# Where the exponentials of two softmax pairs stand on ScalarE, in the prompt tiles of a hybrid decoder layer

## The reference

```python
h = _rms_norm(x, p['ln_mix_pre'])
qa, ka, va, qkvb, bb, ab, zb, qc, gates = jnp.split(h @ p['w_in'], _split_points(), axis=-1)
oa, new_wk, new_wv = swa_fn(qa, ka, va)                       # window attention with sinks, 8 heads of 64
ob, new_conv, new_rec = _gdn_branch(qkvb, bb, ab, zb, ...)    # gated DeltaNet, 4 heads of 128
oc = _mem_attend(qc, mem_k, mem_v)                            # attention to 256 memory rows, 4 heads of 128
gate = jax.nn.sigmoid(gates.reshape(Bsz, L, N_BRANCH, D_MODEL))
mix = jnp.sum(gate * up, axis=2) @ p['w_out']
x = x + _rms_norm(mix, p['ln_mix_post'])
...                                                           # then a SwiGLU feed-forward part
```

## Time and profile before

| | |
|---|---|
| median of 3 runs | 2065.21 us |
| the runs | 2065.07, 2065.21, 2067.7 us |
| the profiled execution | 2062.75 us |
| its span, first to last instruction | 2060.9 us |
| mean granted TensorE clock, as a share of full speed | 0.997 |
| TensorE busy | 2002.7 us (97% of the span) |
| VectorE busy | 987.8 us (48%) |
| ScalarE busy | 517.7 us (25%) |
| GpSimd busy | 742.3 us (36%) |

### The profile page before, as it was taken

One profiled execution on the slowest core, in us unless ns is written; L12 is line 12 of the kernel. 1 busy time (PEld: TensorE's weight loads), 2 busy tenths in 40 slices (PEclk: granted clock), 3 DMA queues, 4 the chain that ended last, 5 costly groups with the idle time before them and its releaser, 6 DMA issues.

```text
span 2060.9 us, 36132 instructions
## 1 busy us (share of the span) xinstructions
PE 2002.7 (97%) x14350; PEld 1903.8 (92%) x14350; DVE 987.8 (48%) x1761; ACT 517.7 (25%) x1151; POOL 742.3 (36%) x318
## 2 busy tenths in 40 slices
PE   6999999999999999999999999999999999999998
PEld 6999999888888889989799888999999999999997
DVE  6755630356565555322459745434353525253535
ACT  5333621243343444321232333100000000000002
POOL 3434774222111122123145322443434343434344
PEclk9999999999999999999999999999999999999999
DMA  5223333433233332263674421111111111111114
GB/s 189 92 83 100 109 114 99 146 105 88 61 99 88 100 91 68 78 190 120 204 247 159 150 104 67 42 51 41 51 41 51 41 51 41 51 41 51 41 41 179
DMA packets 221294, 193.91 MB, mean 94 GB/s; under 512 B 24731, under 2 KB 192283, under 8 KB 221170
## 3 DMA queue, kind: packets, MB, share of 16 engines
q1 hardware_dynamic: 207058, 182.72, 28.7%
q10 hardware_dynamic: 14128, 9.65, 1.6%
HBM read 146.26 MB, written 47.09 MB: 94 GB/s over the span
## 4 chain that ended last, share of the span: by engine, by line
PE 91%; DVE 3%; DMA 2%; ACT 1%; issue 1%; SPq 1%; POOL 0%; ACTq 0%; DVEq 0%; POOLq 0%
PE psum L1508 24%; PE psum L995 13%; PE psum L1569 11%; PE psum L1200 9%; PE psum L1523 5%; PE psum L1500 4%; PE psum L1278 4%; PE psum L1112 3%; PE psum L1247 2%; PE psum L1183 1%; PE psum L1236 1%; PE psum L1019 1%; PE psum L1060 1%; PE psum L1186 1%; ACT pr L1846 1%
## 5 line engine op out<-in xcount | busy, mean ns | idle before, releaser
L853 POOL TENSOR_TENSOR wsp<-raw,kc 128x1024 fp32r<-128x1024 f32 x115 | 279.5, 2430 | 1101.6 <-PE psum L1200 391.6
L1508 PE MATMUL psum<-actD,wsp 128*128 128x352 f32 x3168 | 515.8, 323 | 1.0 <-ACT sg L2052 0.6
L1508 PEld LDWEIGHTS psum<-actD,wsp 128*128 128x128 f32 x3168 | 509.0, 188 | 1.6 <-issue 0.9
L856 POOL TENSOR_TENSOR wsp<-raw,wsp 128x1024 fp32r<-128x1024 f32 x115 | 283.7, 2467 | 9.0
L995 PE MATMUL psum<-actT,wsp 128*128 128x352 f32 x1656 | 269.6, 323 | 0.0
L2640 DVE TENSOR_TENSOR accT<-accT,psum 128x352 f32<-128x352 f32 x504 | 241.7, 520 | 50.1 <-PE psum L1569 50.1
L995 PEld LDWEIGHTS psum<-actT,wsp 128*128 128x128 f32 x1656 | 264.8, 188 | 0.3
L1569 PE MATMUL psum<-fT,wsp 128*128 128x352 f32 x1512 | 249.8, 323 | 0.4 <-DVE accT L2640 0.4
L1569 PEld LDWEIGHTS psum<-fT,wsp 128*128 128x128 f32 x1512 | 244.0, 188 | 0.7 <-DVE accT L2640 0.7
L1200 PE MATMUL psum<-actT,wsp 128*128 128x352 f32 x1152 | 229.6, 338 | 0.0
L2623 DVE TENSOR_TENSOR fr<-psum,sg 128x352 f32<-128x352 f32 x66 | 34.5, 524 | 375.3 <-PE psum L1508 373.1
(11 more groups left out here) (452 smaller groups left out, 2484.8 us busy)
## 6 DMA issues: line engine op xcount, KB each, us to landing
raw<-in_w_in SPq DMA_DIRECT2D x100, 256.0 KB, 4.0
raw<-in_w_ffn_in SPq DMA_DIRECT2D x88, 256.0 KB, 3.1
gat<-s_gate SPq DMA_DIRECT2D x12, 1056.0 KB, 5.0
raw<-in_w_ffn_out SPq DMA_DIRECT2D x44, 256.0 KB, 2.7
s_gate<-gst SPq DMA_DIRECT2D x48, 176.0 KB, 1.9
s_qkv<-y SPq DMA_DIRECT2D x12, 528.0 KB, 3.0
brw<-s_br SPq DMA_DIRECT2D x3, 2112.0 KB, 9.5
raw<-in_w_branch SPq DMA_DIRECT2D x24, 256.0 KB, 5.6
```

Of the source, the lines that this page charges most:

```text
L853: pool.tensor_tensor(wsp[:, slot, 0], raw[:, slot], ones.unsqueeze(1).to_broadcast([P, KT, P]), ALU.mult).then_inc(w_hi, 1)
L856: pool.tensor_tensor(wsp[:, slot, 1], raw[:, slot], wsp[:, slot, 0].bitcast(F32), ALU.subtract).then_inc(w_lo, 1)
L1508: mm = pe.matmul(psum[:, bank, 0:CH], wsp[:, slot, a, k, :], actD[:, h, k, CH * c:CH * c + CH], start=(k == 0 and q == 0), stop=(k == KT - ...
```

## The change

The exponentials of an S step get a step of their own, `("Z", j)`, and `act_tile` issues them there. `TILE` gets six Z steps. Z0, Z3, Z4 and Z5 stand directly behind S0, S3, S4 and S5. Z1 stands behind Y1, Z2 behind Y4. No other engine has a branch for Z. Of the tuple, the part with Z1 and Z2 (before with -, after with +):

```diff
-            ... "INV", ("G", 8), ("E", 0), ("S", 1), ("Y", 1), ("G", 4),
-            ("X", 1), ("G", 3), ("Y", 2), ("T", 1), ("X", 2), ("G", 3), ("Y", 3), ("V", 1), ("X", 3), ("S", 2), ("Y", 4), ("G", 4),
-            ("X", 4), ("G", 3), ("Y", 5), ("T", 2), ("X", 5), ...
+            ... "INV", ("G", 8), ("E", 0), ("S", 1), ("Y", 1),
+            ("Z", 1), ("G", 4), ("X", 1), ("G", 3), ("Y", 2), ("T", 1), ("X", 2), ("G", 3), ("Y", 3), ("V", 1), ("X", 3), ("S", 2),
+            ("Y", 4), ("Z", 2), ("G", 4), ("X", 4), ("G", 3), ("Y", 5), ("T", 2), ("X", 5), ...
@@ act_tile
                     if j == 0:
                         copy((a_vt, t + 1), vtok[:].rearrange("p a d -> p (a d)"), psum[:, 4, 0:2 * P], a_vc)
+                elif step[0] == "Z":
+                    j = step[1]
                     act.wait_ge(a_nm, 6 * t + j + 1)
                     for a in range(2):
                         mm = act.activation(pr[:, a, :], pr[:, a, :] if j < 4 else psum[:, 3, 256 * a:256 * a + 256], ACT.Exp, scale=A_SC[j],
```

More of the change, by code:

```diff
@@ L277, in build @@
     gs_st = [sem(f"gs_st{c}") for c in range(3)]
-    TILE = ("KV", "DEC", ("S", 0), "KK", ("G", 12), ("T", 0), ("G", 8), ("V", 0), "INV", ("G", 8), ("E", 0), ("S", 1), ("Y", 1), ("G", 4),
[5 rows of a table removed]
+    TILE = ("KV", "DEC", ("S", 0), ("Z", 0), "KK", ("G", 12), ("T", 0), ("G", 8), ("V", 0), "INV", ("G", 8), ("E", 0), ("S", 1), ("Y", 1),
[6 rows of a table added]
     assert sum(step[1] for step in TILE if step[0] == "G") == 144
```

## The result

The changed kernel takes 2041.41 us (median of 4 runs, 2037.44 to 2044.71), the kernel before 2065.64 (4 runs): a ratio of 0.988, 95% interval 0.986 to 0.990, 24.2 us less. A second job with the same program, further down, had 2043.59 against 2065.87.

A forecast was written before the change was run, and what follows sets the result against it. TensorE was taken to bound the prompt tiles, standing for ScalarE's Y copies; gains of 1.08 and 1.67 us, 2.75 a tile, 22.0 in eight tiles, took the median 2065.21 to 2043.2 us, range 2039.5 to 2047.5.

The forecast's parts named there:

- What bounds it: Prompt tiles: TensorE sets the pace; its one wait entry is 16 waits, 20.9 us, at X for ScalarE's Y copy.
- When the copy runs: ScalarE at Y1 and Y4: the copy starts 0.73 us after its Y step's first matmul.
- When X starts: TensorE at X1 and X4: starts 0.07 us before the gate block's modelled end, gaining 1.08 and 1.67 us.
- The bounds of 0.91 and 0.73: X1 and X4 starts after the gate block's start: low gain 20.9 us, high gain 23.8 us.
- What the exponentials cost: Moved exponentials on ScalarE: cost nothing, with 1.5 us of slack before T1 and 1.0 us before T2.
- What is late next: VectorE's subtraction after X: stands ready by 1.6 us at X1 and 1.0 us at X4.
- once-a-tile producer: Loads and weight splits at tile boundaries: follow a tile 2.75 us shorter; giving the gain back (2065) had chance 0.04.
- The sum: Whole kernel: 22.0 us less, 2040.7 from the profiled execution and 2043.2 from the median of three runs.
- The range: Whole kernel: 2039.5 to 2047.5 us, from bounds 2041.4 and 2044.3 with 2.6 us of spread each side; chance 0.85.

The follow-up runs named there:

- each half alone: Kernel before with only pair 1's exponentials moved behind the Y1 copy: 2056.06 us; with only pair 2's moved behind the Y4 copy: 2050.12 us.
- four extra copies: Changed kernel with four extra VectorE copies from PSUM ahead of the maxima of pairs 1 and 2: 2042.77 us.
- only pair 2 moved: Kernel before with only pair 2's exponentials put behind the copy of Y4, pair 1 left as before: 2050.12 us, ratio 0.9919.
- only pair 1 moved: Kernel before with only pair 1's exponentials put behind the copy of Y1, pair 2 left as before: 2056.06 us, ratio 0.9953.
- earlier logits: Kernel before, exponentials still ahead of the copies, with pair 1's logits four gate matmuls earlier: 2062.12 us, ratio 0.9984.
- the two with extra VectorE copies: Changed kernel with extra VectorE copies from PSUM ahead of the maxima of pairs 1 and 2: two copies 2041.06 us, four copies 2042.77 us.
- the short blocks: Changed kernel with one gate matmul instead of four between Y1 and X1 and between Y4 and X4, three moved behind X: 2045.81 us.
- the joined pair: Changed kernel with V2 replacing the gate block between X5 and Y6, pair 3's logits directly behind X6: 2037.52 us, again 2038.99 us.

## Why the prediction was right

**What bounds it.** Right. TensorE's list had one entry, and with it gone the stage is TensorE's own work, 448.64 of 449.00 us.

**When the copy runs.** 0.73 us after its Y's first matmul was computed, 0.73 to 0.74 measured. The copy is no slower beside the maxima (0.38 and 0.39).

**When X starts.** 0.84 us after the gate block's start was computed for both (577.45 - 576.61 and 588.10 - 587.26), and 0.84 is what the trace shows at levels 1 and 4 of one tile. The bounds of 0.91 and 0.73 (the block's modelled end, and the block that keeps its form) were both wide of it. The tile's period fell by 2.74 us (59.60 to 56.86) where 2.75 was computed, and each half alone gave its own share.

**What the exponentials cost.** Nothing, as computed: 1.0 us of slack before T2 was computed and 1.0 measured (before T1 1.5 and 1.6). The place after the next Y copy, where that slack is gone, gives the whole gain back.

**What is late next.** The subtraction after X4 stands ready by 0.97 us (1.0 computed), and four extra copies show it to be the next to wait for. No once-a-tile producer became late.

**The sum.** 2043.2 was 1.8 us above the first median, 24.2 us of gain against 22.0. The second comparison, within one job, gave 22.3. What the prediction left out is the clock: it took TensorE's waits at their length alone. In the kernel before some waits are followed by a fall of the clock that costs 1.4 us more, and in the changed kernel's tiles there is none. The profiled execution before had one of these, which is why its tiles came out 23.4 us longer than the changed kernel's and not 22.0. How many the other executions had is not known, and the spread of the runs is larger than 2.2 us, so that the clock is the difference between 24.2 and 22.0 is not shown.

**The range.** The bounds 2041.4 and 2044.3 with 2.6 us on both sides give 2038.8 to 2046.9, not the 2039.5 to 2047.5 that is written; the result lies in both. The spread of 2.6 us that was read from three runs was too small: in the later jobs the kernel before ran between 2060.1 and 2071.12 us (41 runs), and the changed kernel's own first four between 2037.44 and 2044.71. That the median came within 1.8 us is in part luck; the period is the reading that shows the mechanism.

## What to carry to other kernels

When the busiest engine waits for a short copy on an engine that is mostly idle, look at what stands ahead of the copy in that engine's order and what that in turn waits for; a copy that is ready should go ahead of work that is not, as long as the displaced work still ends before its own reader's turn. Compute that slack from the trace for each place, since here one level further back lost all of it. A wait that is taken away can be worth more than its length, and the profile's clock column by microseconds tells where the clock fell; the period of a repeated stage, with and without a fall, tells what it cost.

## What the runs showed of the hardware

TensorE's granted clock can fall after waits of 1.5 us. These counts are from one profiled execution of each kernel. In the tiles, after the 16 waits of 1.0 us (kernel before, and the one with only pair 2 moved) it never fell; after those of 1.6 it fell 1 time in 8, 1 in 8 and 3 in 8 (kernel before, only pair 1 moved, earlier logits); after those of 1.47 us 3 times in 16; after those of 1.68 and 2.26 us, both in each tile, 12 times in 16. A Y or X step of small 64x64 products stands directly ahead of or behind each of these waits. In the seven profiled executions without such waits (the changed kernel twice, the two with extra VectorE copies, the short blocks, the joined pair twice) it never fell in the tiles. Each fall went to 0.50 for 3.4 us and made its tile 1.4 to 1.5 us longer; why that is less than the 1.7 of the clock column is open. So 10.6 us of longer waits came out as 24 us of time. The Trainium skill, TensorE: Matmul & The Clock Gate, in its part on the clock gate, has the same two levels, 2.4 GHz and 1.2 GHz; the traces agree with them (1.00 and 0.50).

Falls also happen with TensorE busy throughout, as at 82 and 164 us above. Both began within 1.3 us after a run of 18 matmuls with one column each (79.14 to 81.06 and 162.01 to 163.93 us); other executions passed the same place without a fall, so what starts those is open.
